# A routed SwiGLU layer on one core: in positions of 64 seats, the down product one block later and the gated tile's halves half a block later

## The chip, the cores and the metric

The kernel runs on one core of a Trainium2 chip. The metric is the device time in microseconds of that core, the median of several runs. The engines are TensorE (PE; its weight loads are PEld), VectorE (DVE), ScalarE (ACT), GpSimd (POOL) and SyncE (SP), which issues the weight loads from HBM.

## The reference

Two layers of an encoder on 256 tokens of width 1024, in f32. The second layer ends in a mixture of experts, and this is where the change lies:

```python
def swiglu(h, w1, w3, w2):
    return (jax.nn.silu(h @ w1) * (h @ w3)) @ w2

def moe_swiglu(h, w_router, w1, w3, w2):
    logits = (h @ w_router).astype(jnp.float32)
    top_v, top_i = lax.top_k(logits, TOP_K)          # TOP_K = 2 of 8 experts
    wts = jax.nn.softmax(top_v, axis=-1)
    combine = jnp.sum(jax.nn.one_hot(top_i, N_EXPERTS, dtype=jnp.float32) * wts[..., None], axis=-2)
    out = jnp.zeros_like(h)
    for e in range(N_EXPERTS):
        out = out + combine[..., e:e + 1] * swiglu(h, w1[e], w3[e], w2[e])
    return out
```

Each expert has w1 and w3 of 1024 x 3584 and w2 of 3584 x 1024, 42 MB together, and all eight are read once.

## The kernel before

**Precision.** Every weight and every activation is split in two f32r parts: a high part (rounded) and a low part (what is left). A product is then three: high x high, low activation x high weight, high activation x low weight. The weights stream through 1 MB items: SP loads an item into one of seven slots of `raw`, ScalarE copies it to `whi` (L1727, "the split"), VectorE subtracts to `wlo` (L2352, "the low part"). `whi` and `wlo` have three slots each. ScalarE may split item n when TensorE is done with item n-3, and SP may load into a slot when VectorE has made the low part of the item that was in it.

**Positions and blocks.** The eight experts are worked on in eight positions, with the roles "HLHLHLHH". A heavy position (H) has 128 seats (rows of tokens); a light one (L) has 64, and goes to an expert with few tokens. In a light position the high and the low part of the rows lie side by side in the 128 columns of one tile. So one pass with the high weights does two products at once, and the sum of the two halves is made later by a matmul with `fold`. Each position has seven blocks (`NM` = 7) of 512 columns of the hidden width. A block has six items: w1 (two halves), w3 (two halves), w2 (two halves).

**One block on the engines.** TensorE (`blocks`) does the up product with w1 of block b into bank 0 (L1188 with the high part of the weights, L1192 with the low part), then `hidden_T` of block b-1, then the up product with w3 of block b into bank 1, then `down` of block b-1 (L1231) into banks 4 and 5. `hidden_T` brings the hidden tile of a block to the layout that the down product wants: in heavy positions by transposes (L1211), in light ones by matmuls with `fold` (L1207) which also add the halves. ScalarE copies bank 0 to SBUF (L1738: silu in heavy positions, plain in light ones). VectorE makes the product with bank 1 in heavy positions (L2366) or copies bank 1 (L2363) in light ones.

In light positions the gate is formed after the fold, so there are four more small steps per block on the tile of 128 x 256: silu (ScalarE, `silu_folded`, L1743), the gated product (VectorE, L2377), its high part (ScalarE, L1749) and its low part (VectorE, L2380; the trace names its output yT_hi, which holds both parts). There is one `silu_t` and one `gated_t`; `gated_m`, where the parts go, has two buffers, taken in turn by blocks. In heavy positions the parts are made straight from the bank (L1753, L2385).

**What sets the order.** Each engine runs the order written out for it in its own section; there is no planner at run time. Items come in the order of `e_items`: `head_items` (w1 and w3 of block 0), `mid_items` (w1, w3 of block b and w2 of block b-1), and w2 of the last block, which comes behind the head of the next position. On ScalarE and VectorE, `e_hi(e_room(...))` and `e_lo(e_room(...))` put ahead of a small step just those items whose slot is free before TensorE reaches the named product. ScalarE also gathers and stores: at block 4 it issues the load of the next position's rows (L1794), VectorE and ScalarE split these rows at block 6 (L1763, L2397), and the result of a position goes out from ScalarE (L1777); after a light position it is folded first, in block 1 of the next (L1243, L1771). An overflow loop, which runs only where an expert has more tokens than its seats, uses the heavy form and did not run here.

Of the kernel before, what the change touches and what calls it, by code (L numbers as in the profile page):

```python
# [33 lines left out]
F32 = mybir.dt.float32  # L34
# [212 lines left out]
def build(nc, x, mem, positions, g_mix, w_in, g_q, g_kv, w_uq, w_uk, w_uv, g_sg, w_s, b_s, g_mem,  # L247
# [31 lines left out]
    with ExitStack() as ctx:  # L279
# [284 lines left out]
            return w[0, :, b, half, :, :, :][e, :, :, :].rearrange("k p c -> p k c")  # L564


        def halves(p, *blocks):
            return [(p, kind, b, half) for kind, b in blocks for half in range(2)]

        def head_items(p):  # L570
            return halves(p, ("w1", 0), ("w3", 0))

        def mid_items(p):
            return [i for b in range(1, NM) for i in halves(p, ("w1", b), ("w3", b), ("w2", b - 1))]

        e_items = head_items(0)
        for p in range(NE):
            e_items += mid_items(p) + (head_items(p + 1) if p < LAST else []) + halves(p, ("w2", NM - 1))
        N_E = len(e_items)
        PER_E = N_E // NE  # L580
        HEAD = len(head_items(0))
# [96 lines left out]
        def e_room(phase, kind, n):  # L678

            limit = marks[phase, kind, n][0]  # L680
            start, end = (N_E, N_E + PER_E) if phase == "over" else (0, N_E)
            i = start + SPLIT
            while i < end and marks["item", i - SPLIT][0] < limit:
                i += 1
            return i
# [13 lines left out]
        def _(pe):  # L699
# [464 lines left out]
                k = 2 if e_items[n][1] == "w2" else 4  # L1164
                return tile[:, (E0 + n) % SPLIT, :].rearrange("p (k c) -> p k c", k=k)

            def is_light(phase):
                return phase != "over" and light[phase]

            def up(phase, kind, b_, j=0, rows=None):  # L1170

                name = {"w1": "e1", "w3": "e3"}[kind]
# [81 lines left out]
            def blocks(phase, j=0):  # L1254

                for b_ in range(1, NM):
                    up(phase, "w1", b_, j)
                    if b_ == 1 and phase != "over" and phase and light[phase - 1]:
                        fold_result(phase - 1)
                    hidden_T(phase, b_ - 1, j)  # L1260
                    if phase != "over" and phase < LAST and b_ == NM - 1:

                        pe.wait_ge(slots_moved, 32 * phase + 16)
                        rows_T(phase + 1)
                    up(phase, "w3", b_, j)
                    if phase == LAST and b_ == NM - 1:
                        down(phase, b_ - 1, j, (0,))
                        hidden_T(phase, b_, j)
                        down(phase, b_ - 1, j, (1,))
                    else:  # L1270
                        down(phase, b_ - 1, j)
                    if phase == LAST and b_ == 2:
                        select_T(phase, j)

# [26 lines left out]
            for p in range(NE):  # L1301
                blocks(p)
                if p < LAST:
                    up(p + 1, "w1", 0, 0, lambda half: read(pe, (p + 1, "rows", half)))
                    hidden_T(p, NM - 1)
                    up(p + 1, "w3", 0)
                    down(p, NM - 1)
            combine(LAST)
            marks["over"] = [count, 0]
# [168 lines left out]
        def _(act):  # L1478
# [239 lines left out]
            def e_hi(end, j=0):  # L1718

                nonlocal n_done  # L1720
                for n in range(n_done, end):
                    act.wait_ge(raw_in[n % RAW], e_base[n % RAW] + 16 * (n // RAW + 1) + 16 * (PER_E // RAW) * j)
                    if N_E <= n < N_E + SPLIT:
                        reached(act, "over", j)
                    else:
                        reached(act, ("item", n - SPLIT), j)
                    nc.scalar.activation(whi[:, (E0 + n) % SPLIT, :], raw[:, n % RAW, :], ACT.Copy).then_inc(hi_ready, 1)  # L1727
                n_done = max(n_done, end)

            def is_light(phase):  # L1730
                return phase != "over" and light[phase]

            def e_silu(phase, b_, j=0):

                b = full(act, (phase, "e1", b_), j)
# [43 lines left out]
            def blocks(phase, j=0):  # L1779

                for b_ in range(1, NM):
                    e_hi(e_room(phase, "e1", b_), j)
                    if is_light(phase):
                        e_hi(e_room(phase, "eT", b_ - 1), j)
                        silu_folded(phase, b_ - 1)
                    e_silu(phase, b_, j)
                    if b_ == 1 and phase != "over" and phase and light[phase - 1]:
                        store_result(phase - 1)
                    if phase != "over" and phase < LAST and b_ == 4:

                        act.wait_ge(dispatched, 16 * 2 * T)
                        if phase:
                            reached(act, (phase, "rows", 1))
                        act.dma_start(row_in_slot, rows_by_slot[phase + 1]).then_inc(slots_moved, 16)  # L1794
                    e_hi(e_room(phase, "eT", b_ - 1), j)
                    hidden_hi(phase, b_ - 1, j)
                    if phase == LAST and b_ == 3:
                        select_T(phase, j)

# [20 lines left out]
            for p in range(NE - 1):  # L1820
                blocks(p)

                e_hi(e_room(p, "e3", NM - 1))
                reached(act, (p, "e3", NM - 1))
                rows_hi_part(p + 1)
                e_hi(e_room(p + 1, "e1", 0))
                if light[p]:
                    e_hi(e_room(p, "eT", NM - 1))
                    silu_folded(p, NM - 1)
                e_silu(p + 1, 0)  # L1830
                e_hi(e_room(p, "eT", NM - 1))
                hidden_hi(p, NM - 1)
                e_hi(e_room(p, "ey", 0))

                act.wait_ge(slots_moved, 32 * p + 16)
                for n in range(2):
                    b = full(act, (p, "ey", n))
                    free(nc.scalar.activation(y_slot[:, n * HALF:(n + 1) * HALF], b[:, :], ACT.Copy), (p, "ey", n))
                if not light[p]:
                    store_result(p)  # L1840
# [25 lines left out]
        def _(dve):  # L1866
# [486 lines left out]
                                    ALU.subtract).then_inc(lo_ready, 1)  # L2353
                n_done = max(n_done, end)

            def is_light(phase):
                return phase != "over" and light[phase]

            def hidden(phase, b_, j=0):

                b = full(dve, (phase, "e3", b_), j)
# [3 lines left out]
                read(dve, (phase, "e1", b_), j)  # L2365
                free(V.tensor_tensor(g32_m, silu_m, b[:, :], ALU.mult), (phase, "e3", b_))  # L2366

            def hidden_lo(phase, b_, j=0):

                end = N_E + PER_E if phase == "over" else N_E  # L2370
                last = phase in (LAST, "over") and b_ == NM - 1
                e_lo(min(e_room(phase, "eT", b_), end - 1 if last else end), j)
                b = full(dve, (phase, "eT", b_), j)
                count = NM * (NE if phase == "over" else phase) + b_ + 1 + NM * j
                if is_light(phase):
                    dve.wait_ge(silu_t_ready, light_block(phase, b_))
                    free(V.tensor_tensor(gated_t, silu_t, b[:, BM * LIGHT:2 * BM * LIGHT], ALU.mult), (phase, "eT", b_))  # L2377
                    dve.wait_ge(g_hi, count)
                    part = by_slot(gated_m[0][:, b_ % 2, :])
                    V.tensor_tensor(part[:, :, LIGHT:2 * LIGHT], gated_t.rearrange("p (c s) -> p c s", c=BM),  # L2380
                                    part[:, :, 0:LIGHT].bitcast(F32), ALU.subtract).then_inc(g_lo, 1)
                    return
                dve.wait_ge(g_hi, count)
                part = [v[:, b_ % 2, :] for v in gated_m]
                free(V.tensor_tensor(part[1], b[:, :], part[0].bitcast(F32), ALU.subtract), (phase, "eT", b_))  # L2385

# [33 lines left out]
            def blocks(phase, j=0):  # L2420

                for b_ in range(1, NM):
                    e_lo(e_room(phase, "e1", b_), j)
                    hidden_lo(phase, b_ - 1, j)
                    e_lo(e_room(phase, "e3", b_), j)
                    if phase != "over" and phase < LAST and b_ == NM - 1:
                        rows_lo(phase + 1)
                    hidden(phase, b_, j)
                    if phase == LAST and b_ == 1:
                        last_choice()  # L2430
                    if phase == LAST and 2 <= b_ <= 5:
                        add_picked(b_ % T, (b_ - 2) // T)
# [22 lines left out]
            for p in range(NE - 1):  # L2455
                blocks(p)
                e_lo(e_room(p + 1, "e1", 0))
                hidden_lo(p, NM - 1)
                e_lo(e_room(p + 1, "e3", 0))
                hidden(p + 1, 0)  # L2460
            dve.wait_ge(flag_ready, 1)
            overflow = dve.value_load(more[0:1, 0:1], min_val=0, max_val=1)
            blocks(LAST)
# [67 lines left out]
```

## Time and profile before

| | |
|---|---|
| median of 3 runs | 1665.05 us (1664.66 to 1665.84) |
| profiled execution | 1664.9 us |
| its span | 1663.1 us |
| PE busy | 1582.4 us (95%) |
| DVE busy | 1286.1 us (77%) |
| ACT busy | 1054.5 us (63%) |
| loaded and stored by DMA | 497.48 MB, mean 299 GB/s |
| weight items of the routed layer | 336 of 1 MB, about 720 us to the end |

The span is the time from the first to the last instruction; the execution lies around it. Busy PE is modelled: matmuls overlap, so a busy engine is not one at its peak. The three light positions lie at about 827 to 945, 1063 to 1181 and 1299 to 1418 us of the span.

### The profile page before, as it was taken

To read this page: it belongs to the slowest core of one execution; us is meant where nothing else is said; L and a number is where in the kernel's file an instruction comes from. 1 tells how busy PE (TensorE), PEld (TensorE's weight loads), DVE (VectorE), ACT (ScalarE), POOL (GpSimd) and SP (SyncE) were. 2 spreads that over 40 slices of the span, in tenths; PEclk is the share of its full clock that TensorE was granted. 3 is DMA by queue.
4 is the path that set the end of the run, shared out by engine and by line. 5 is a ranking of instruction groups with operands and counts; after the bars stand their busy time and mean duration, and the time that the engine had idled before them with its cause. 6 is when DMAs were issued, how large, how long until landed. Compare 5 with 4: busy or idle time off the path is not lost.

```text
span 1663.1 us, 21020 instructions
## 1 busy us (share of the span) xinstructions
PE 1582.4 (95%) x8224; PEld 1332.9 (80%) x8224; DVE 1286.1 (77%) x1204; ACT 1054.5 (63%) x988; POOL 32.4 (2%) x69
## 2 busy tenths in 40 slices
PE   9999999999999999999987999888999888999997
PEld 8988889999899888878766788766788667788885
DVE  7575667555567747698988888898888888888997
ACT  6554436433465544567777777777777777777775
POOL 1000000000000000020000000000000000000100
PEclk9999999999999999999999999999999999999998
DMA  7753488886365444699999999999999999999993
GB/s 234 242 180 121 151 278 282 269 264 190 103 200 198 139 139 165 253 350 409 379 388 396 371 386 388 375 375 404 370 380 374 393 383 384 381 389 366 389 404 121
DMA packets 186120, 497.48 MB, mean 299 GB/s; under 512 B 8534, under 2 KB 64400, under 8 KB 186016
## 3 DMA queue, kind: packets, MB, share of 16 engines
q1 hardware_dynamic: 180016, 479.23, 78.5%
q0 software_dynamic: 2624, 8.45, 1.5%
q10 hardware_dynamic: 3376, 8.39, 1.3%
q8 instruction: 68, 1.11, 0.3%
q14 instruction: 36, 0.29, 0.1%
HBM read 476.64 MB, written 19.40 MB: 298 GB/s over the span
## 4 chain that ended last, share of the span: by engine, by line
PE 65%; DVE 22%; ACT 6%; issue 4%; DMA 1%; SPq 0%; ACTq 0%; POOL 0%; DVEq 0%; POOLq 0%
PE bank L731 20%; DVE wlo L2352 16%; PE bank L1188 12%; PE bank L1231 12%; PE bank L902 9%; PE bank L1192 6%; ACT whi L1727 3%; ACT whi L1494 1%; PE bank L721 1%; DVE wlo L1908 1%; PE bank L1016 1%; PE bank L1211 1%; DMA x_sb<-in_x 1%; DVE sgv L2363 1%; DMA hn<-in_mem 1%
## 5 line engine op out<-in xcount | busy, mean ns | idle before, releaser
L2352 DVE TENSOR_TENSOR wlo<-raw,whi 128x2048 fp32r<-128x2048 f32 x328 | 740.8, 2286 | 96.7 <-ACT whi L1727 96.0
L1727 ACT ACTIVATE whi<-raw 128x2048 fp32r<-128x2048 f32 x328 | 621.6, 1914 | 141.4 <-PE bank L1231 69.3
L1908 DVE TENSOR_TENSOR wlo<-raw,whi 128x2048 fp32r<-128x2048 f32 (+3 forms) x121 | 259.2, 2147 | 176.1 <-ACT whi L1494 174.1
L1188 PE MATMUL bank<-whi,yT_hi 128*128 128x512 f32 x896 | 312.6, 397 | 0.0
L1494 ACT ACTIVATE whi<-raw 128x2048 fp32r<-128x2048 f32 (+3 forms) x121 | 217.7, 1801 | 141.9 <-PE bank L731 100.8
L1192 PE MATMUL bank<-wlo,yT_hi 128*128 128x512 f32 x896 | 243.5, 394 | 4.1 <-DVE wlo L1908 2.8
L1231 PE MATMUL bank<-whi,yT_hi 128*128 128x512 f32 x448 | 180.1, 402 | 57.5 <-DVE wlo L2352 30.7
L1188 PE MATMUL bank<-whi,yT_lo 128*128 128x512 f32 x560 | 217.2, 391 | 0.0
L1192 PEld LDWEIGHTS bank<-wlo,yT_hi 128*128 128x128 f32 x896 | 166.0, 188 | 48.7 <-DVE wlo L2352 10.5
L1188 PEld LDWEIGHTS bank<-whi,yT_hi 128*128 128x128 f32 x896 | 167.0, 188 | 33.4
L1231 PE MATMUL bank<-wlo,yT_hi 128*128 128x512 f32 x448 | 175.8, 392 | 0.0
L1231 PEld LDWEIGHTS bank<-whi,yT_hi 128*128 128x128 f32 x448 | 84.3, 188 | 93.1 <-ACT whi L1727 33.2
L731 PE MATMUL bank<-hT_hi,whi 128*128 128x256 f32 x464 | 131.4, 283 | 0.0
L731 PE MATMUL bank<-hT_hi,wlo 128*128 128x256 f32 x464 | 131.3, 283 | 0.0
L731 PE MATMUL bank<-hT_lo,whi 128*128 128x256 f32 x464 | 131.3, 283 | 0.0
L1188 PEld LDWEIGHTS bank<-whi,yT_lo 128*128 128x128 f32 x560 | 105.5, 189 | 21.3 <-DVE yT_lo L2291 0.2
L1231 PE MATMUL bank<-whi,yT_lo 128*128 128x512 f32 x280 | 109.0, 389 | 0.0
L1231 PEld LDWEIGHTS bank<-wlo,yT_hi 128*128 128x128 f32 x448 | 84.6, 189 | 16.8
L731 PEld LDWEIGHTS bank<-hT_lo,whi 128*128 128x128 f32 x464 | 89.0, 192 | 0.4
L731 PEld LDWEIGHTS bank<-hT_hi,whi 128*128 128x128 f32 x464 | 89.0, 192 | 0.4
L731 PEld LDWEIGHTS bank<-hT_hi,wlo 128*128 128x128 f32 x464 | 89.0, 192 | 0.0
L731 PE MATMUL bank<-whi,mT_hi 128*128 128x512 f32 (+1 forms) x204 | 79.6, 390 | 0.1
(323 smaller groups left out, 2065.9 us busy)
## 6 DMA issues: line engine op xcount, KB each, us to landing
raw<-in_moe_w SPq DMA_DIRECT2D x336, 1024.0 KB, 7.0
raw<-in_w_in SPq DMA_DIRECT2D x36, 1024.0 KB, 5.2
raw<-in_dense_w SPq DMA_DIRECT2D x30, 1024.0 KB, 6.5
raw<-in_w_br SPq DMA_DIRECT2D x12, 1024.0 KB, 5.0
rows_by_slot<-qxT SPq DMA_DIRECT2D x23, 512.0 KB, 7.3
raw<-in_w_out SPq DMA_DIRECT2D x8, 1024.0 KB, 5.0
raw<-in_w_mkv SPq DMA_DIRECT2D x6, 1024.0 KB, 8.3
cqkv<-rows_by_slot ACTq DMA_DIRECT2D x7, 512.0 KB, 6.9
```

Of the source, the lines that this page charges most:

```text
L721: ins = nc.tensor.matmul(bank, lhs(k), rhs(k), start=(k == 0), stop=(k == n - 1))
L731: ins = nc.tensor.matmul(bank, lhs(a, k), rhs(b, k), start=(start and k == chunks[0] and a + b == 0), stop=(stop and k == chunks[-1] and a ...
L902: ins = nc.tensor.matmul(bank, src(a, x0), w[b_][:, w0, :], start=(start and q + i == 0), stop=(stop and last))
L1016: ins = nc.tensor.matmul(b[:, t * SEQ:(t + 1) * SEQ], qT[0:QK, h, tok(t)], kT[0:QK, h, :], start=True, stop=True)
L1188: nc.tensor.matmul(b[:, :], hselT[a][:, half, tok(k)], w[:, k, :], start=(half + k + a == 0), stop=False)
L1192: ins = nc.tensor.matmul(b[:, :], hselT[0][:, half, tok(k)], w[:, k, :], start=False, stop=(half == 1 and k == 3))
L1211: ins = nc.tensor.transpose(b[:, tok(c)], g32_m[:, tok(c)], ident[:, :])
L1231: ins = nc.tensor.matmul(banks[4 + n][:, :], gated_m[a][:, b_ % 2, tok(2 * half + c)], w[p][:, c, n * HALF:(n + 1) * HALF], start=(b_ + ha ...
L1494: nc.scalar.activation(whi[:, m % SPLIT, 0:floats(n)], raw[:, pieces[n][1], 0:floats(n)], ACT.Copy).then_inc(hi_ready, 1)
L1727: nc.scalar.activation(whi[:, (E0 + n) % SPLIT, :], raw[:, n % RAW, :], ACT.Copy).then_inc(hi_ready, 1)
L1908: V.tensor_tensor(wlo[:, m % SPLIT, 0:size], raw[:, pieces[n][1], 0:size], whi[:, m % SPLIT, 0:size].bitcast(F32), ALU.subtract).then_inc( ...
L2352: V.tensor_tensor(wlo[:, s, :], raw[:, n % RAW, :], whi[:, s, :].bitcast(F32), ALU.subtract).then_inc(lo_ready, 1)
```

## The change

Everything is in light positions. The items of w2 come one block later in `e_items`: w2(b-2) behind w1(b) and w3(b), and at the end of the position w2(5) and w2(6) behind the head of the next. TensorE follows: `down` of block b-2 at the end of block b, none at the end of block 1, and two at the end of the position. On ScalarE the high part of the gated tile of block b-2 is made in block b, behind the splits of w1 and w3 and ahead of the silu of block b-1. On VectorE `hidden_lo` is taken apart: `gated_lo` (the low part) of block b-2 is made in block b behind the low parts of w1 and w3, and `gated` (the product) of block b-1 at the end of block b, ahead of the copy of bank 1. The number of instructions and their shapes stay as they were. `is_light` is moved up, so that all engines share it.

```diff
         def mid_items(p):
-            return [i for b in range(1, NM) for i in halves(p, ("w1", b), ("w3", b), ("w2", b - 1))]
+            lag = 2 if is_light(p) else 1
+            return [i for b in range(1, NM)
+                    for i in halves(p, ("w1", b), ("w3", b), *([("w2", b - lag)] if b >= lag else []))]
+
+        def tail_items(p):
+            return halves(p, *([("w2", NM - 2)] if is_light(p) else []), ("w2", NM - 1))
...
-            e_items += mid_items(p) + (head_items(p + 1) if p < LAST else []) + halves(p, ("w2", NM - 1))
+            e_items += mid_items(p) + (head_items(p + 1) if p < LAST else []) + tail_items(p)
...
@@ TensorE, blocks
-                    else:
+                    elif not is_light(phase):
                         down(phase, b_ - 1, j)
+                    elif b_ > 1:
+                        down(phase, b_ - 2)
@@ TensorE, end of a position
                     up(p + 1, "w3", 0)
+                    if light[p]:
+                        down(p, NM - 2)
                     down(p, NM - 1)
@@ ScalarE, blocks
                     if is_light(phase):
-                        e_hi(e_room(phase, "eT", b_ - 1), j)
+                        if b_ > 1:
+                            hidden_hi(phase, b_ - 2)
+                        e_hi(e_room(phase, "eT", b_ - 1))
                         silu_folded(phase, b_ - 1)
...
-                    hidden_hi(phase, b_ - 1, j)
+                    if not is_light(phase):
+                        hidden_hi(phase, b_ - 1, j)
@@ ScalarE, end of a position
                 if light[p]:
+                    hidden_hi(p, NM - 2)
                     e_hi(e_room(p, "eT", NM - 1))
                     silu_folded(p, NM - 1)
                 e_silu(p + 1, 0)
-                e_hi(e_room(p, "eT", NM - 1))
+                e_hi(e_room(p + 1, "e3", 0) if light[p] else e_room(p, "eT", NM - 1))
                 hidden_hi(p, NM - 1)
@@ VectorE
+            def gated(p, b_):
+
+                b = full(dve, (p, "eT", b_))
+                dve.wait_ge(silu_t_ready, light_block(p, b_))
+                if light_block(p, b_) > 1:
+                    dve.wait_ge(g_lo, light_block(p, b_) - 1)
+                free(V.tensor_tensor(gated_t, silu_t, b[:, BM * LIGHT:2 * BM * LIGHT], ALU.mult), (p, "eT", b_))
+
+            def gated_lo(p, b_):
+
+                dve.wait_ge(g_hi, NM * p + b_ + 1)
+                part = by_slot(gated_m[0][:, b_ % 2, :])
+                V.tensor_tensor(part[:, :, LIGHT:2 * LIGHT], gated_t.rearrange("p (c s) -> p c s", c=BM),
+                                part[:, :, 0:LIGHT].bitcast(F32), ALU.subtract).then_inc(g_lo, 1)
@@ VectorE, blocks
                     e_lo(e_room(phase, "e1", b_), j)
-                    hidden_lo(phase, b_ - 1, j)
+                    if not is_light(phase):
+                        hidden_lo(phase, b_ - 1, j)
+                    elif b_ > 1:
+                        gated_lo(phase, b_ - 2)
                     e_lo(e_room(phase, "e3", b_), j)
                     if phase != "over" and phase < LAST and b_ == NM - 1:
                         rows_lo(phase + 1)
+                    if is_light(phase):
+                        gated(phase, b_ - 1)
                     hidden(phase, b_, j)
@@ VectorE, end of a position
                 e_lo(e_room(p + 1, "e1", 0))
-                hidden_lo(p, NM - 1)
+                if light[p]:
+                    gated_lo(p, NM - 2)
+                else:
+                    hidden_lo(p, NM - 1)
                 e_lo(e_room(p + 1, "e3", 0))
+                if light[p]:
+                    gated(p, NM - 1)
                 hidden(p + 1, 0)
+                if light[p]:
+                    gated_lo(p, NM - 1)
```

## Rows read from the trace of the kernel before

**Rows 1.** The page and the groups of instructions: busy, mean ns, idle before
```profile
span 1663.1 us, 21020 instructions
PE 1582.4 (95%) x8224; PEld 1332.9 (80%) x8224; DVE 1286.1 (77%) x1204; ACT 1054.5 (63%) x988; POOL 32.4 (2%) x69
...
L1727 ACT ACTIVATE whi<-raw 128x2048 fp32r<-128x2048 f32 x328 | 621.6, 1914 | 141.4 <-PE bank L1231 69.3 <-PE bank L1192 66.8 <-issue 1.8
```

**Rows 2.** Timeline of VectorE, one light block: start, duration, instruction, [idle before it]
```profile
861.35 0.68 DVE L2363 COPY sgv<-bank 128x512 f32<-128x512 f32 x1
861.95 11.09 DVE L2352 TENSOR_TENSOR wlo<-raw,whi 128x2048 fp32r<-128x2048 f32 x5
872.96 0.41 DVE L2377 TENSOR_TENSOR cT<-cT,bank 128x256 f32<-128x256 f32 x1
873.85 0.43 DVE L2380 TENSOR_TENSOR yT_hi<-cT,yT_hi 128x256 fp32r<-128x256 f32 x1 [0.48 <-ACT yT_hi L1749]
875.66 2.29 DVE L2352 TENSOR_TENSOR wlo<-raw,whi 128x2048 fp32r<-128x2048 f32 x1 [1.38 <-ACT whi L1727]
...
889.47 0.41 DVE L2377 TENSOR_TENSOR cT<-cT,bank 128x256 f32<-128x256 f32 x1
```

**Rows 3.** Timeline of ScalarE in the same block
```profile
867.78 1.91 ACT L1727 ACTIVATE whi<-raw 128x2048 fp32r<-128x2048 f32 x1 [0.26 <-PE bank L1192]
869.60 0.36 ACT L1743 ACTIVATE cT<-bank 128x256 f32<-128x256 f32 x1
...
873.40 0.42 ACT L1749 ACTIVATE yT_hi<-cT 128x256 fp32r<-128x256 f32 x1 [2.95 <-DVE cT L2377]
```

**Rows 4.** Timeline of TensorE in the same block, from w1 half 1 on
```profile
866.49 1.19 PE L1192 MATMUL bank<-wlo,yT_hi 128*128 128x512 f32 x4
867.52 1.89 PE L1207 MATMUL bank<-cT,sgv 128*128 128x64 f32 x16
...
871.16 1.08 PE L1188 MATMUL bank<-whi,yT_hi 128*128 128x512 f32 x4
...
874.33 0.50 PE L1231 MATMUL bank<-whi,yT_hi 128*128 128x512 f32 x1 [1.19 <-DVE yT_hi L2380]
```

**Rows 5.** The group of L2380 over the whole span
```profile
L2380 DVE TENSOR_TENSOR yT_hi<-cT,yT_hi 128x256 fp32r<-128x256 f32 x21 | 8.9, 425 | 10.1 <-ACT yT_hi L1749 10.1
```

**Rows 6.** Windows: length, busy (instructions) by engine, PEclk, DMA share, GB/s
```profile
717.00:734.00 17.00, 17.00 (x78) 14.06 (x77) 14.96 (x9) 12.68 (x9) 1.51 (x1) 1.00 1.02 417
734.00:751.00 17.00, 17.00 (x79) 14.05 (x78) 14.95 (x9) 12.67 (x9) 0.00 (x0) 1.00 1.03 410
...
853.00:870.00 17.00, 14.11 (x67) 10.89 (x66) 15.14 (x10) 12.74 (x12) 0.00 (x0) 1.00 1.00 366
```

**Rows 7.** Timeline of VectorE, one heavy block, from its L2385 to the next
```profile
740.28 0.68 DVE L2385 TENSOR_TENSOR yT_lo<-bank,yT_hi 128x512 fp32r<-128x512 f32 x1
...
757.08 0.68 DVE L2385 TENSOR_TENSOR yT_lo<-bank,yT_hi 128x512 fp32r<-128x512 f32 x1
```

**Rows 8.** Timeline of VectorE, start of the first light position
```profile
833.31 6.70 DVE L2352 TENSOR_TENSOR wlo<-raw,whi 128x2048 fp32r<-128x2048 f32 x3 [1.49 <-ACT whi L1727]
```

**Rows 9.** Timeline of VectorE, block 6 of the first light position
```profile
927.41 1.28 DVE L2397 TENSOR_TENSOR yT_lo<-bank,yT_hi 128x512 fp32r<-128x512 f32 x2
```

**Rows 10.** Timeline of TensorE, end of the first light position
```profile
927.64 0.47 PE L1231 MATMUL bank<-whi,yT_hi 128*128 128x512 f32 x1 [1.65 <-DVE wlo L2352]
...
929.56 0.40 PE L1188 MATMUL bank<-whi,yT_hi 128*128 128x512 f32 x1
...
939.85 0.39 PE L1188 MATMUL bank<-whi,yT_hi 128*128 128x512 f32 x1
...
942.57 0.39 PE L1231 MATMUL bank<-whi,yT_hi 128*128 128x512 f32 x1
...
947.28 0.39 PE L1188 MATMUL bank<-whi,yT_hi 128*128 128x512 f32 x1
```

**Rows 11.** Weight loads issued between 820 and 828 us
```profile
DMA to landing us min/median/max: 6.8/7.1/7.9
```

More of the change, by code:

```diff
@@ L564, in e_source, with is_light @@
             return w[0, :, b, half, :, :, :][e, :, :, :].rearrange("k p c -> p k c")
+        def is_light(phase):
+            return phase != "over" and light[phase]
         def halves(p, *blocks):
@@ L1165, in e_part @@
                 return tile[:, (E0 + n) % SPLIT, :].rearrange("p (k c) -> p k c", k=k)
-            def is_light(phase):
-                return phase != "over" and light[phase]
             def up(phase, kind, b_, j=0, rows=None):
@@ L1728, in e_hi @@
                 n_done = max(n_done, end)
-            def is_light(phase):
-                return phase != "over" and light[phase]
             def e_silu(phase, b_, j=0):
@@ L2354, in e_lo @@
                 n_done = max(n_done, end)
-            def is_light(phase):
-                return phase != "over" and light[phase]
             def hidden(phase, b_, j=0):
@@ L2373, in hidden_lo @@
                 b = full(dve, (phase, "eT", b_), j)
[L2374 to L2383, printed above, removed]
+                dve.wait_ge(g_hi, NM * (NE if phase == "over" else phase) + b_ + 1 + NM * j)
                 part = [v[:, b_ % 2, :] for v in gated_m]
```

## The prediction

> **What bounds the kernel now.** I read the page first: 1663.1 us of span, TensorE busy 95% [rows 1]. That is a mean over stages. Then I read the VectorE timeline of one block of a 64-seat position, because the change touches only those. The reader sees there, per block, six low-part instructions, a copy, the gated product (L2377) and its low part (L2380), and two pauses: 0.48 us before L2380 and 1.38 us before the next low part [rows 2]. From the gated product to the next one it is 16.51 us (872.96 to 889.47). The work in it is 6 x 2.202 (11.01 for five, start to start) + 0.60 + 0.41 + 0.43 = 14.65 us, and the pauses are the other 1.86.
>
> The ScalarE timeline says why [rows 3]: it stands 2.95 us before L1749, for L2377; then comes 0.42 of high part and then a weight split of 1.9 us, for which VectorE waits. Nothing else holds that split: TensorE had been done with the item three before it since 871.2 [rows 4]. So two engines hand one tile to and fro in order, and the next weight item queues behind it on ScalarE. TensorE stands too, 1.19 us for L2380 [rows 4] and 1.65 us for the low part (the same wait stands first in [rows 10]), once each per block: here it follows, it does not set the pace. The pattern is the same 21 times; L2380's wait sums to 10.1 us [rows 5]. In positions of 128 seats TensorE is busy for the whole of a 17 us window [rows 6] and a block takes 16.80 us [rows 7], so these set their own pace and hand on any gain of a light position unshortened.
>
> **The change part by part.** Nothing is added or removed in number: 42 items per position, the same products, the same three small tiles per block. Moved are, in light positions: the down product of block b to block b+2's end, L2380's counterpart to half a block later, ScalarE's high part the same, and the gated product to the end of the block. SP's loads follow the new item order, one for one; POOL has nothing here.
>
> *Steady block.* VectorE would run: 4 low parts, low part of g(b-2), 2 low parts, gated product of b-1, copy of b. ScalarE's high part of g(b-2) now needs a product that VectorE made at the end of the block before, so it never waits; the 2.95 and both pauses go. Three followers could be late next. (a) The gated product needs the silu of the folded tile: ready at 869.96 in this block [rows 3], needed after the sixth low part, at about 875.6: hidden. (b) The split of the sixth item, w2 half 1, needs TensorE done with w3 half 0. The low part of w1 half 1 ends at 861.95 + 2 x 2.202 = 866.35; TensorE then does its last quartet, the fold, and w3 half 0, done at 871.16 [rows 4]; ScalarE starts 0.26 after such an end (867.52 to 867.78) and takes 1.92: 873.34. VectorE wants it after 3 low parts and one small one, at 866.35 + 6.61 + 0.43 = 873.39. Slack 0.05 us: it fits and no more. I price it at nothing; the other end is a wait per block of whatever the estimate misses, for which the nearest row is a handoff of 0.26, 15 blocks, 4 us. (c) The ring of raw slots, below. TensorE is busy 14.1 us of 17 in such blocks [rows 6], or 13.7 of 16.51, which fits in 14.65. So a steady block takes 14.65.
>
> *Start of a light position.* Up to the three low parts at 833.31 nothing changes [rows 8]. Then w3(1) twice and w1(2) twice end at 833.31 + 8.81 = 842.12; gated 0, copy 1: 843.13; w3(2) twice, low part of g(0), w2(0) twice: 852.37; gated 1, copy 2: 853.38. Three blocks: copy 5 ends at 897.3. The low part of w2(4) half 1 ends at 897.3 + 13.21 + 0.43 = 911.0. Before, the same place in the code (last low part ahead of the two row parts, L2397) ended at 927.41 [rows 9]; 16.4 earlier, with two items fewer done, 4.40, and one small instruction.
>
> *End of a light position.* TensorE started the second half of the down product at 927.64, 0.15 us after its low part, and the next position's w1 at 929.56 [rows 10]. After: 911.1 and 913.0, 16.5 earlier. Up products and fold of a 128-seat head then run with no gap on TensorE, 929.56 to 942.57 = 13.0 us, so to 926.0. Now two more halves of down product stand here, w2(5): VectorE's low part of the first is done at 911.0 + 1.2 (rows) + 0.41 + 0.60 + 8.81 + 0.43 + 2.2 = 924.6, that of the second, whose split must wait for w3' half 0 (939.85 - 16.5 = 923.3) and takes 1.92, at 927.6; TensorE does both by 929.8. The last gated product keeps the old handoff: gated 6 at 927.6 to 928.0, ScalarE's high part to 928.4, and only then its split of w2(6) half 0, to 930.3; low part to 932.6. The product of the next position's block 0 and the low part of g(6), 1.03 us, lie inside that wait. TensorE stands from 929.8 to 932.7 (2.9 us), does half 0 to 934.6, waits 0.3 for half 1 and ends at 936.8. Before, this point was 947.28 [rows 10]. **Gain 10.4 us per light position, 31.2 for three**: of 7 x 1.86 = 13.0 us of pauses per position about 2.6 stay or come back at the end. Bounds: 6 x 1.86 = 11.2 if the end costs only its pause, so 33.6 in all; and 8 if that end costs a further low part of 2.3.
>
> *The loads.* A light block moves 6 x 1.0486 = 6.29 MB; in 14.65 us that asks 429 GB/s. With many loads under way, in the stretch from 717 on, the rows show 417 and 410 GB/s [rows 6], so a block alone would need 6.29 / 0.410 = 15.3 us. The ring of seven slots can cover this for a time. From 827.1 (two low parts, 2 x 2.3, ahead of the 1.49 us of wait in [rows 8]) to 911.0 VectorE frees 34 slots; with a result store and a row load of 0.52 MB that is 36.7 MB in 83.8 us; at 410 GB/s it takes 89.5. Loads fall behind by 5.7 us. A load landed in 7.1 us when the position began [rows 11] and may take 14.65 - 1.94 - 0.2 = 12.5 before ScalarE is late (a slot is wanted again one block later, less the split). 7.1 + 5.7 = 12.8: the ring runs dry just as the position ends, 0.3 us short. The next position, at TensorE's pace (6.29 MB in 16.8 us, 374 GB/s), fills it again. At 417 it is never dry; at 405, my lower guess between rows, 1.4 us per position. I take 0.3 x 3 = 1 us, range 0 to 4.5.
>
> The page DMA: Bandwidth & Descriptors of the Trainium skill (Where 436 GB/s comes from) says that loads from HBM are held by the HBM side at about 358 GB/s per core. The rows contradict it for this core alone: 410 over a whole window [rows 6]. Another section of that page (Bandwidth) has 425 GB/s for one core alone and large transfers; by it an estimate is 36.7 / 0.425 = 86.4 us and a ring that never dries, 1 us better than my sum.
>
> **Sum**: 31.2 - 1 = 30.2 us. The profiled execution took 1664.9 us (1.8 outside its span), the median of the runs is 1665.05, 0.15 more, which changes nothing; so 1664.9 - 30.2 = **1634.7 us**, 1.8% less.
>
> **Rivals.**
> A. *The chain of (b) is late.* Each block then waits for its sixth split. For it: slack of 0.05 us only. Against: every time in it is a row of an undisturbed block. Price 0.3 to 1.0 us x 15 blocks: 1639 to 1650, at its middle 1644.
> B. *The loads take the place of the pauses.* If the ring gives less cover than I reckon (bursts with gaps), all of 15.3 per block stands: 0.7 x 15 = 10 us back, 1645, and with the store and the row load up to 5.7 x 3 = 17, 1651. For it: the loads' share is full in all windows. Against: of the 141.4 us that ScalarE's splits waited, 137.9 are put down by name and none to a load [rows 1], and the ring held landings of 7 us where 12.5 are allowed.
> C. *Slower than before.* In the window 853 to 870 the rate was 366 GB/s at a full share [rows 6]. Were that what the memory gives to this order of loads, and not what was asked for, 36.7 MB would take 100.3 us against 83.8, 16.5 lost against 10.4 won, and 128-seat blocks (6.29 / 0.366 = 17.2 us) would not refill the ring: 1665 + 3 x 6 = 1683. It decides below 36.7 / (83.8 + 10.4) = 390 GB/s. Against: 410 to 417 held from 717 to 751, two blocks. The 358 GB/s of the Trainium skill's page would have this effect too.
> D. *The change does nothing*: the high part waits as before, because the new order on VectorE meets the old point on ScalarE. Price 0: 1665. Against: the code puts the product a half block and four splits ahead of its reader.
>
> **How the numbers follow.** Forecast (31 us within a few) 0.70; A 0.10; B 0.12; C 0.04; D 0.02; 0.02 for something unnamed on either side. Low end: 33.6 won and no load wait, 1631.4, less 1.4 for sizes: 1630. High end: takes in most of B and the middle of A, 1647. 0.2% of 1665 is 3.3 us, about what a measurement here tells from no change. Faster: forecast, A, B and half the unnamed, 0.93; same: D and a part of C, 0.03; slower: 0.04.
>
> **What would show it.** Right: in light positions VectorE's timeline shows six low parts, gated, copy in 14.65 us, no wait before L2380's counterpart, no wait of ScalarE for the gated product except at the end of the position; there TensorE waits some 2.9 us before the last down product (and the end of its last down product, at 947.28 [rows 10], moves to 936.8). Landings grow through a light position to 11 or 12 us. Wrong: a wait of VectorE for the sixth split (A), ScalarE waiting for raw (B or C), 128-seat blocks over 16.8 us.

## The result and the profile after

The changed kernel takes 1638.67 us in the median (1636.11 to 1639.41, 4 runs) against 1665.44 us for the kernel before, measured alongside it: a ratio of 0.9837, 95% interval 0.982 to 0.9854, 26.8 us less. I had said 1634.7 and 1630 to 1647. The traced execution has a span of 1636.6 us against 1663.1.

The VectorE timeline of a light block, answering [rows 2] (start, duration, instruction, [idle before]; L2362 is the low part of a weight item, L2381 the gated product, L2387 its low part, L2370 the copy of bank 1):

```profile
865.03 0.42 DVE L2381 TENSOR_TENSOR cT<-cT,bank 128x256 f32<-128x256 f32 x1
865.36 0.69 DVE L2370 COPY sgv<-bank 128x512 f32<-128x512 f32 x1
865.96 8.89 DVE L2362 TENSOR_TENSOR wlo<-raw,whi 128x2048 fp32r<-128x2048 f32 x4
874.76 0.42 DVE L2387 TENSOR_TENSOR yT_hi<-cT,yT_hi 128x256 fp32r<-128x256 f32 x1
875.10 4.55 DVE L2362 TENSOR_TENSOR wlo<-raw,whi 128x2048 fp32r<-128x2048 f32 x2
879.56 0.41 DVE L2381 TENSOR_TENSOR cT<-cT,bank 128x256 f32<-128x256 f32 x1
```

No row has an idle time: both pauses of [rows 2] are gone, and a block takes 14.53 us (865.03 to 879.56) where it took 16.51. My figure was 14.65. A block of a 128-seat position behind it takes 16.82 us (967.64 to 984.46, both at L2398, VectorE's low part there), as before.

What is left stands in block 6 and at the end of a position. The same timeline, answering [rows 9], then ScalarE's last high part, which answers to the 2.95 us of [rows 3]:

```profile
907.29 2.29 DVE L2362 TENSOR_TENSOR wlo<-raw,whi 128x2048 fp32r<-128x2048 f32 x1 [0.82 <-ACT whi L1736]
909.50 1.28 DVE L2410 TENSOR_TENSOR yT_lo<-bank,yT_hi 128x512 fp32r<-128x512 f32 x2
...
924.49 2.29 DVE L2362 TENSOR_TENSOR wlo<-raw,whi 128x2048 fp32r<-128x2048 f32 x1 [1.44 <-ACT whi L1736]
926.70 0.42 DVE L2381 TENSOR_TENSOR cT<-cT,bank 128x256 f32<-128x256 f32 x1
927.03 0.68 DVE L2373 TENSOR_TENSOR sgv<-sgv,bank 128x512 f32<-128x512 f32 x1
927.63 0.42 DVE L2387 TENSOR_TENSOR yT_hi<-cT,yT_hi 128x256 fp32r<-128x256 f32 x1
929.41 6.70 DVE L2362 TENSOR_TENSOR wlo<-raw,whi 128x2048 fp32r<-128x2048 f32 x3 [1.36 <-ACT whi L1736]
```
```profile
927.15 0.42 ACT L1755 ACTIVATE yT_hi<-cT 128x256 fp32r<-128x256 f32 x1 [2.69 <-DVE cT L2381]
```

TensorE's timeline at the end of the first light position, answering [rows 10] (L1236 is the down product; L1193 at 938.40 is the first matmul of the up product that follows), and the same place in the second:

```profile
931.84 0.77 PE L1236 MATMUL bank<-whi,yT_hi 128*128 128x512 f32 x1 [2.82 <-DVE wlo L2362]
932.41 0.63 PE L1236 MATMUL bank<-wlo,yT_hi 128*128 128x512 f32 x1
...
938.40 0.39 PE L1193 MATMUL bank<-whi,yT_hi 128*128 128x512 f32 x1
...
1161.34 0.47 PE L1236 MATMUL bank<-whi,yT_hi 128*128 128x512 f32 x1 [2.82 <-DVE wlo L2362]
1161.65 0.40 PE L1236 MATMUL bank<-wlo,yT_hi 128*128 128x512 f32 x1
...
1165.47 0.39 PE L1193 MATMUL bank<-whi,yT_hi 128*128 128x512 f32 x1
```

The wait is 2.82 us; the working gave 2.9. But what follows it takes 6.56 us in the first position (931.84 to 938.40) and 4.13 in the second, for the same sixteen matmuls. The windows (columns as in [rows 6]) show why: in the first, TensorE's granted clock was 0.50, the lower of its two levels.

```profile
932.00:936.00 4.00, 4.00 (x10) 3.13 (x11) 4.00 (x2) 1.28 (x2) 0.00 (x0) 0.50 1.03 411
...
1162.00:1166.00 4.00, 3.87 (x18) 2.88 (x17) 4.00 (x3) 2.96 (x4) 0.00 (x0) 1.00 1.03 411
```

**Where the 26.5 us of the two traces are.** A mark in both is the first low part behind the wait of 1.48 or 1.49 us in block 1 of a light position (833.31 before, [rows 8]) and, behind the third position, the one after a wait of 3 us. Before, the last three of the four marks:

```profile
1069.60 6.70 DVE L2352 TENSOR_TENSOR wlo<-raw,whi 128x2048 fp32r<-128x2048 f32 x3 [1.48 <-ACT whi L1727]
...
1305.81 6.70 DVE L2352 TENSOR_TENSOR wlo<-raw,whi 128x2048 fp32r<-128x2048 f32 x3 [1.48 <-ACT whi L1727]
...
1430.22 2.29 DVE L2352 TENSOR_TENSOR wlo<-raw,whi 128x2048 fp32r<-128x2048 f32 x1 [3.10 <-ACT whi L1727]
```

After, all four:

```profile
831.58 8.90 DVE L2362 TENSOR_TENSOR wlo<-raw,whi 128x2048 fp32r<-128x2048 f32 x4 [1.49 <-ACT whi L1736]
...
1060.66 8.90 DVE L2362 TENSOR_TENSOR wlo<-raw,whi 128x2048 fp32r<-128x2048 f32 x4 [1.48 <-ACT whi L1736]
...
1287.72 8.90 DVE L2362 TENSOR_TENSOR wlo<-raw,whi 128x2048 fp32r<-128x2048 f32 x4 [1.48 <-ACT whi L1736]
...
1403.79 2.29 DVE L2362 TENSOR_TENSOR wlo<-raw,whi 128x2048 fp32r<-128x2048 f32 x1 [3.04 <-ACT whi L1736]
```

The lead grows from 1.73 to 8.94, 18.09 and 26.43 us: 7.2, 9.15 and 8.3 us per light position, 24.7 in all. The first 1.73 lie ahead of anything that the change touches. TensorE's clock was granted at 0.89 in 706 to 722 us of the trace before and at 1.00 in that of after. The control e6 below is the changed kernel run once more. It has 0.89 there again, and its first mark lies at 833.22 us, so these 1.73 us belong to the execution and not to the change. Its marks:

```profile
833.22 8.90 DVE L2362 TENSOR_TENSOR wlo<-raw,whi 128x2048 fp32r<-128x2048 f32 x4 [1.49 <-ACT whi L1736]
...
1059.95 8.90 DVE L2362 TENSOR_TENSOR wlo<-raw,whi 128x2048 fp32r<-128x2048 f32 x4 [1.48 <-ACT whi L1736]
...
1287.92 8.90 DVE L2362 TENSOR_TENSOR wlo<-raw,whi 128x2048 fp32r<-128x2048 f32 x4 [1.49 <-ACT whi L1736]
...
1404.01 2.29 DVE L2362 TENSOR_TENSOR wlo<-raw,whi 128x2048 fp32r<-128x2048 f32 x1 [3.20 <-ACT whi L1736]
```

Here the three positions give 9.56, 8.24 and 8.32 us, 26.1 in all.

### The profile page after: what moved, and what is told of

The parts are those of the page before. It is cut to its first block, busy times and chain, and to the rows that moved or that the text cites. A ratio compares the mean times of both kernels' runs of the same rounds, so it can differ in the third digit from the quotient of the medians.

```text
span 1636.6 us, 21020 instructions
## 1 busy us (share of the span) xinstructions
PE 1585.5 (97%) x8224; PEld 1334.3 (82%) x8224; DVE 1284.8 (79%) x1204; ACT 1057.1 (65%) x988; POOL 31.9 (2%) x69
## 4 chain that ended last, share of the span: by engine, by line
PE 71%; DVE 18%; ACT 5%; issue 4%; DMA 2%; ACTq 0%; POOL 0%; DVEq 0%; SPq 0%; POOLq 0%
PE bank L739 21%; PE bank L1193 14%; PE bank L1236 13%; DVE wlo L2362 12%; PE bank L910 9%; PE bank L1197 8%; ACT whi L1736 2%; ACT whi L1503 1%; PE bank L729 1%; DVE wlo L1918 1%; PE bank L1024 1%; DMA raw<-in_moe_w 1%; PE bank L1216 1%; PE bank L1212 1%; DVE sgv L2370 1%
## 5 line engine op out<-in xcount | busy, mean ns | idle before, releaser
L2362 DVE TENSOR_TENSOR wlo<-raw,whi 128x2048 fp32r<-128x2048 f32 x328 | 742.6, 2287 | 82.3 <-ACT whi L1736 81.5
L1736 ACT ACTIVATE whi<-raw 128x2048 fp32r<-128x2048 f32 x328 | 625.3, 1917 | 166.2 <-PE bank L1197 76.5
L1193 PE MATMUL bank<-whi,yT_hi 128*128 128x512 f32 x896 | 312.0, 396 | 0.0
L1193 PE MATMUL bank<-whi,yT_lo 128*128 128x512 f32 x560 | 216.5, 390 | 0.0
L1236 PE MATMUL bank<-whi,yT_hi 128*128 128x512 f32 x448 | 181.0, 404 | 26.3 <-DVE wlo L2362 20.7
L1193 PEld LDWEIGHTS bank<-whi,yT_hi 128*128 128x128 f32 x896 | 166.7, 188 | 33.3
L1236 PE MATMUL bank<-wlo,yT_hi 128*128 128x512 f32 x448 | 177.3, 396 | 0.0
L1236 PEld LDWEIGHTS bank<-whi,yT_hi 128*128 128x128 f32 x448 | 85.7, 191 | 59.8 <-issue 29.7
L1193 PEld LDWEIGHTS bank<-whi,yT_lo 128*128 128x128 f32 x560 | 105.2, 188 | 21.2 <-DVE yT_lo L2301 0.2
L1236 PE MATMUL bank<-whi,yT_lo 128*128 128x512 f32 x280 | 109.0, 389 | 0.0
L1236 PEld LDWEIGHTS bank<-wlo,yT_hi 128*128 128x128 f32 x448 | 85.7, 191 | 17.2
```

The costliest lines, as they stand in the source:

```text
L1193: nc.tensor.matmul(b[:, :], hselT[a][:, half, tok(k)], w[:, k, :], start=(half + k + a == 0), stop=False)
L1236: ins = nc.tensor.matmul(banks[4 + n][:, :], gated_m[a][:, b_ % 2, tok(2 * half + c)], w[p][:, c, n * HALF:(n + 1) * HALF], start=(b_ + ha ...
L2362: V.tensor_tensor(wlo[:, s, :], raw[:, n % RAW, :], whi[:, s, :].bitcast(F32), ALU.subtract).then_inc(lo_ready, 1)
```

## The experiments

Theory H: what went is a handoff. VectorE's gated product, ScalarE's high part and VectorE's low part follow each other in order, and ScalarE's next split is queued behind the high part. Rival P: what went is TensorE's wait for the down product. For the part of the forecast that is missing, the candidates are the loads (L) and TensorE's clock (K). The experiments are called e1 to e8.

**e1: the down product late, alone.** ScalarE and VectorE keep the order they had before; items and TensorE have the new one.

```diff
@@ ScalarE, light block
-                        if b_ > 1:
-                            hidden_hi(phase, b_ - 2)
...
-                    if not is_light(phase):
-                        hidden_hi(phase, b_ - 1, j)
+                    hidden_hi(phase, b_ - 1, j)
...
@@ VectorE, light block
-                    elif b_ > 1:
-                        gated_lo(phase, b_ - 2)
+                    else:
+                        e_lo(e_room(phase, "eT", b_ - 1))
+                        gated(phase, b_ - 1)
+                        gated_lo(phase, b_ - 1)
...
-                    if is_light(phase):
-                        gated(phase, b_ - 1)
...
```

> Only the down product is one block later (and its items and the two at the end); the gated product, its high part and its low part stay together at the place they had in the kernel before. Theory H (the gain is the handoff between VectorE and ScalarE, with the next split queued behind the high part): VectorE still pauses 0.48 and 1.38 us per block, a light block stays at 16.5 us, and the time is that of before, 1663 to 1668 us. Theory P (the gain is that TensorE no longer waits 1.19 and 1.65 us for the down product): most of the gain is there, 1640 to 1648 us.

The same is done at the end of a position (not shown).

Measured: 1676.55 us, ratio 1.0066 (1.005 to 1.0081). Theory P falls. H had the pauses right, but neither the time nor the block: it is slower than before, and a block such as the one from 868.28 to 885.52 us takes 17.24 us instead of 16.5. The timelines of VectorE and TensorE:

```profile
885.52 0.42 DVE L2377 TENSOR_TENSOR cT<-cT,bank 128x256 f32<-128x256 f32 x1
886.42 0.42 DVE L2383 TENSOR_TENSOR yT_hi<-cT,yT_hi 128x256 fp32r<-128x256 f32 x1 [0.48 <-ACT yT_hi L1755]
888.23 2.29 DVE L2358 TENSOR_TENSOR wlo<-raw,whi 128x2048 fp32r<-128x2048 f32 x1 [1.38 <-ACT whi L1736]
...
896.46 2.29 DVE L2358 TENSOR_TENSOR wlo<-raw,whi 128x2048 fp32r<-128x2048 f32 x1 [0.94 <-ACT whi L1736]
```
```profile
890.67 0.77 PE L1236 MATMUL bank<-whi,yT_hi 128*128 128x512 f32 x1 [2.83 <-DVE wlo L2358]
891.23 0.63 PE L1236 MATMUL bank<-wlo,yT_hi 128*128 128x512 f32 x1
```

The pauses of 0.48 and 1.38 us are there as before. TensorE, whose two waits were 1.19 and 1.65 us [rows 4, 10], now has one of 2.83, about the same in sum. Behind it matmuls lie 0.43 us apart instead of 0.23, and the split that waits for them comes late (0.94). All eleven waits of 2.5 to 2.9 us ahead of the down product in this trace have such slow matmuls behind them, and the mean granted clock of the whole run is 0.982 against 0.995 before. So e1 is not the down product's delay alone: it brings a fall of the clock with it. What it shows is that the delay doesn't remove VectorE's pauses. What the delay would cost or give at the full clock no run shows.

**e2: the late split first, and nothing else.** The kernel before with two lines changed:

```diff
-                    e_hi(e_room(phase, "eT", b_ - 1), j)
+                    e_hi(e_room(phase, "eT", b_ - 1) + is_light(phase), j)
                     hidden_hi(phase, b_ - 1, j)
...
-                e_hi(e_room(p, "eT", NM - 1))
+                e_hi(e_room(p, "eT", NM - 1) + light[p])
                 hidden_hi(p, NM - 1)
```

> The kernel before with one edit: in light positions ScalarE makes one more split (the one that was late) ahead of the high part of the gated tile; nothing is moved on TensorE, VectorE or SP. The slot for it is free in time by the trace of before (871.4 us, the gated product comes at 873.4). Theory H: the pause of 1.38 us goes in all seven handoffs of a position, that of 0.48 stays, a block takes 15.13 us; 1.38 x 21 = 29.0 us less, 1636 to 1640 us, as good as the changed kernel, since at 416 GB/s the loads ask less of the ring. Theory P: TensorE's down product still waits for the low part, so little goes, 1655 us or more.

Measured: 1641.1 us, ratio 0.9854 (0.9839 to 0.9869). So 24.8 us come from one split moved ahead of the high part on ScalarE. VectorE's timeline:

```profile
885.45 0.42 DVE L2377 TENSOR_TENSOR cT<-cT,bank 128x256 f32<-128x256 f32 x1
886.35 0.43 DVE L2380 TENSOR_TENSOR yT_hi<-cT,yT_hi 128x256 fp32r<-128x256 f32 x1 [0.48 <-ACT yT_hi L1749]
886.69 2.28 DVE L2352 TENSOR_TENSOR wlo<-raw,whi 128x2048 fp32r<-128x2048 f32 x1
...
900.50 0.41 DVE L2377 TENSOR_TENSOR cT<-cT,bank 128x256 f32<-128x256 f32 x1
...
917.09 0.43 DVE L2380 TENSOR_TENSOR yT_hi<-cT,yT_hi 128x256 fp32r<-128x256 f32 x1 [1.13 <-ACT yT_hi L1749]
...
934.59 0.42 DVE L2380 TENSOR_TENSOR yT_hi<-cT,yT_hi 128x256 fp32r<-128x256 f32 x1 [1.74 <-ACT yT_hi L1749]
```

A block takes 15.05 us; 1.38 is gone and 0.48 stays, as expected. In the last two handoffs of a position VectorE waits 1.13 and 1.74 us for the high part, 1.91 more than twice 0.48. In three positions that is 5.7 us, enough for the miss of 1 to 5 us.

**e3: the same at the end of the changed kernel's positions.**

```diff
-                e_hi(e_room(p + 1, "e3", 0) if light[p] else e_room(p, "eT", NM - 1))
+                e_hi(e_room(p + 1, "e3", 0) + 1 if light[p] else e_room(p, "eT", NM - 1))
                 hidden_hi(p, NM - 1)
```

> The changed kernel with one edit: at the end of a light position ScalarE makes the split of w2(6) half 0 ahead of the high part of the last gated tile. VectorE's pause of 1.36 us there goes, and TensorE's wait of 2.82 us falls to 1.4. If the last handoff is what keeps the gain at 9 instead of 13 us per position: 1.4 x 3 = 4.3 us less than the changed kernel, and some more if TensorE's clock no longer falls behind the shorter wait (it cost 2.7 and 1.0 us in two of three positions): a ratio to before of 0.9790 to 0.9815, some 1631 to 1635 us. If the loads bound the end of the position (ScalarE then waits for raw instead): no difference from the changed kernel, 1636 to 1639.

Measured: 1632.25 us, ratio 0.9803 (0.9789 to 0.9816), better than the changed kernel. VectorE's pause of 1.36 us is gone, and TensorE waits half as long, without a fall of the clock (1.00 in the windows over all three ends):

```profile
932.37 0.47 PE L1236 MATMUL bank<-whi,yT_hi 128*128 128x512 f32 x1 [1.38 <-DVE wlo L2362]
```

**e4: half of each load.**

```diff
-                sp.dma_start(dst, src).then_inc(raw_in[slot], 16)
+                half = src.shape[1] // 2
+                sp.dma_start(dst[:, :half, :], src[:, :half, :]).then_inc(raw_in[slot], 16)
```

> The changed kernel, but each weight load of the routed layer from position 0 on brings only half of its rows per partition (0.5 MB instead of 1), so that the rest of the slot holds old data; all engines do the same work. Theory L (the loads take back part of the gain at the ends of light positions): ScalarE's waits for raw, 14.8 us in sum in the trace of the changed kernel, go to 0, and 2 to 4 us of time go with them: 1634.5 to 1637. If the loads were hidden even so: no difference, within 1 us of the changed kernel's 1638.7. Were it more than 6 us, my account of the ring would be wrong.

Measured: 1637.93 us, ratio 0.9831 (0.9818 to 0.9845) beside 0.9837: no difference that can be told. In the changed kernel ScalarE does wait for loads, 14.8 us in sum. The loads issued between 1055 and 1140 us, in the second light position, landed in 12.0 us in the median and 13.6 at most, where my working allowed 12.5:

```profile
DMA to landing us min/median/max: 7.6/12.0/13.6
```

ScalarE's splits in the changed kernel, then here:

```profile
L1736 ACT ACTIVATE whi<-raw 128x2048 fp32r<-128x2048 f32 x328 | 625.3, 1917 | 166.2 <-PE bank L1197 76.5 <-PE bank L1236 69.4 <-DMA raw<-in_moe_w 14.8
```
```profile
L1737 ACT ACTIVATE whi<-raw 128x2048 fp32r<-128x2048 f32 x328 | 624.8, 1917 | 165.7 <-PE bank L1197 87.3 <-PE bank L1236 73.1 <-issue 1.6
```

The sum of its waits is the same, 166.2 and 165.7 us. Without the loads it waits for TensorE instead: 145.9 us in the changed kernel (76.5 for the up product and 69.4 for the down product) and 160.4 here. VectorE's pause ahead of the sixth low part of block 6 is still there:

```profile
909.27 2.29 DVE L2363 TENSOR_TENSOR wlo<-raw,whi 128x2048 fp32r<-128x2048 f32 x1 [0.81 <-ACT whi L1737]
```

**e5 and e6: the clock kept up.** Ten idle matmuls in the wait at the end of a light position, and the changed kernel again as a control (e6).

```diff
                         down(p, NM - 2)
+                        for _ in range(10):
+                            nc.tensor.matmul(banks[3][:, 0:P], ident[:, :], ident[:, :], start=True, stop=True)
                     down(p, NM - 1)
```

> The changed kernel with ten more matmuls of 128 columns on TensorE (result unused, into a bank that lies idle) in the wait of 2.8 us ahead of the last down product of each light position. Theory K (that wait brings TensorE's granted clock to its lower level in some positions, 2.7 us lost in the first and 1.0 in the third of the traced run): the granted clock stays 1.00 in 926 to 940 and its like, no matmul of the last down product is 0.43 us apart, and the time is 1 to 3.5 us under the changed kernel in the same call. Theory N (the fall of the clock is not tied to the wait): the clock falls as before and the time is the same or some tenths longer.

> The changed kernel once more, as the control of this call: 1636 to 1639.5 us. What its trace shows of TensorE's clock after the 2.8 us waits tells whether it falls in the same positions each time.

Measured: 1636.46 us (0.9817, 0.9803 to 0.983) against 1638.84 for the control (0.9837, 0.9824 to 0.9851). The intervals overlap, so the 2.4 us alone settle little; the traces say more. The granted clock over the three ends (924 to 944, 1150 to 1172, 1376 to 1400 us) is 1.00, 1.00, 1.00 with the matmuls, 1.00, 0.92, 0.93 in the control and 0.83, 1.00, 0.93 in the first trace of the changed kernel. The second position, with the matmuls and in the control (the granted clock is the third number from the end):

```profile
1150.00:1172.00 22.00, 21.27 (x107) 17.46 (x107) 18.76 (x12) 16.25 (x13) 0.00 (x0) 1.00 1.03 409
```
```profile
1150.00:1172.00 22.00, 19.18 (x75) 14.77 (x74) 17.63 (x11) 14.96 (x11) 0.00 (x0) 0.92 1.03 409
```

With e4 there are nine waits of 2.8 us that stand empty; the clock fell behind six of them, and behind none of the three that the matmuls filled. So the fall is tied to the wait but does not follow every one. In the traced run of e5 VectorE also paused 1.7 and 1.6 us, in bits of 0.2 to 0.5, in blocks 4 to 6 of its first two light positions. In the first of them ScalarE waited for loads:

```profile
ACT whi L1738 <- DMA raw<-in_moe_w: 7.6, 12, 1.9
```

These are 7.6 us in twelve waits between 870 and 915 us, the longest 1.9. So the loads can reach VectorE in one execution and not in another: in the control each light position has only the one pause in block 6 (0.69, 0.58 and 0.81 us).

**e7: the rows' transposes later**, on top of the split at the end.

```diff
-                    if phase != "over" and phase < LAST and b_ == NM - 1:
+                    if phase != "over" and phase < LAST and b_ == NM - 1 and not light[phase]:
...
                     up(phase, "w3", b_, j)
+                    if is_light(phase) and b_ == NM - 1:
+                        pe.wait_ge(slots_moved, 32 * phase + 16)
+                        rows_T(phase + 1)
```

> The changed kernel with the split ahead at the end (as in e3_end_split) and, in light positions, the eight transposes of the next position's rows (0.80 us on TensorE) behind the up product with w3 of block 6 instead of ahead of it. Theory R (the 0.82 us pause of VectorE before the sixth low part of block 6 is my tight chain (b) with these transposes in it): the pause goes, 0.8 x 3 = 2.4 us under e3_end_split, 1629.5 to 1630.5 us at 1665.4 of before. If the pause is the loads (ScalarE waits 0.3 to 0.65 us for raw just there): it stays, and so does the time of e3_end_split, 1632 us.

Measured: 1629.71 us, ratio 0.9787 (0.9774 to 0.9801), 36 us under before and the shortest of the kernels that load all of their weights. The pause ahead of the sixth low part of block 6 is gone; in the first light position (L2413 are the row parts, and the wait of 1.44 us at the end of the position stays):

```profile
906.13 4.55 DVE L2365 TENSOR_TENSOR wlo<-raw,whi 128x2048 fp32r<-128x2048 f32 x2
910.60 1.28 DVE L2413 TENSOR_TENSOR yT_lo<-bank,yT_hi 128x512 fp32r<-128x512 f32 x2
...
925.59 2.29 DVE L2365 TENSOR_TENSOR wlo<-raw,whi 128x2048 fp32r<-128x2048 f32 x1 [1.44 <-ACT whi L1739]
```

The intervals of e3 and e7 overlap, so the traces decide: mark to mark, the three light positions are 0.93, 0.72 and 0.77 us shorter than in e3, 2.4 in all, as Theory R had it.

**e8: and that with half loads**, to see if the loads bind at this pace.

> The kernel of e7_rows_later, but each weight load of the routed layer brings only half of its rows per partition (0.5 MB), so that the rest of the slot holds old data. e7 asks the loads for more than the changed kernel does (its light positions are 2.2 us shorter). Theory L2 (at this pace the ring of slots begins to run dry in some executions, as the spread of e7, 1629.6 to 1631.8, suggests): 0.5 to 2 us less, 1628 to 1629, with a narrower spread. If the loads are hidden here too: 1629.5 to 1630.5.

Measured: 1629.07 us, ratio 0.9782 (0.9769 to 0.9796): 0.0005 under e7, which can't be told from none. Theory L2 is neither shown nor excluded.

## Why the prediction was right, and where it was off

*The handoff, and 14.65 us for a steady block*: right, 14.53. e2 shows the cause: with only the split moved ahead of the high part, 24.8 us go. e1 shows that the down product's delay leaves both pauses where they were. In the changed kernel it is what lets the high part be made half a block later.

*(a), the silu hidden*: right, no wait before L2381.

*(b), the sixth split with 0.05 us of slack, priced at nothing*: right in blocks 2 to 5, wrong in block 6. There TensorE makes the next rows' transposes, 0.80 us, inside the chain, and VectorE paused 0.82. I had reckoned the chain from a block without them. That is rival A in one block of seven. e7 takes it away, for 2.4 us in the traces and 2.5 in the medians.

*The end of a position, 2.9 us of wait and 936.8*: the wait came out at 2.82; the end at 938.40, where 936.8 less the 1.73 of the early start is 935.1. Of these 3.3 us, 2.4 are the slow matmuls behind the wait (6.56 us against 4.13), which no step of mine had. The other 0.9 stand ahead of it: the wait ended at 931.84 us, which is 933.6 with the early start, where I had 932.7. That is about what the pause of 0.82 us in block 6 gives; no run separates the two. I had named the wait, and not what a wait does to the clock, though the trace before had an example. There TensorE waited 2.02 us at the start of the first light position, and slow matmuls (0.63 us instead of 0.39) followed:

```profile
841.30 0.50 PE L1231 MATMUL bank<-whi,yT_hi 128*128 128x512 f32 x1 [2.02 <-DVE yT_hi L2380]
...
842.36 0.63 PE L1231 MATMUL bank<-wlo,yT_hi 128*128 128x512 f32 x1
```

*The loads, 1 us and at most 4.5; rivals B and C*: the mechanism is there, landings of 12.0 us in the median of the second position and ScalarE waiting 14.8 us, but on an engine with time in hand. The medians of e4 and e8 lie 0.0006 and 0.0005 of the ratio, about 1 us, under those of the kernels with whole loads, which is within the intervals. In single traces the price differs: the changed kernel's second position gave 9.15 us, with three pauses of 0.26 to 0.29, and the first two of e5 gave 8.07 and 8.11, against 9.51 in its third; in their blocks 4 to 6 ScalarE waited 7.6 and 7.4 us for loads, in the third 3.4. So in that execution the loads took some 1.4 us twice. B is a matter of 0 to 3 us per execution, not of 10. The loads ran at 409 GB/s over the ends of the light positions (windows of 20 to 24 us), so C, which needed less than 390, falls. The limit of about 358 GB/s that the Trainium skill states for loads from HBM (DMA: Bandwidth & Descriptors, Where 436 GB/s comes from) doesn't hold for this core working alone.

*The sum, 31.2 - 1 = 30.2*: 24.7 and 26.1 in the two traces where the change acts, 26.8 in the medians. The term that was mis-sized is the gain per position, 10.4. Where the clock stayed up and VectorE paused in block 6 alone it was 9.5 or 9.6 (9.56 in e6's first position, 9.55 and 9.51 in the third of e4 and e5). Of the 0.85 us that are missing there, the pause in block 6 is 0.8 by e7. Where the clock fell it was 8.2 to 8.3 in five positions and 7.2 in one. That the steady block was 0.1 us shorter than I had it, some 0.5 us per position, worked the other way, so about as much more is lost in a place that no run shows.

## What to carry to other kernels

When two engines pass a tile to and fro, look at what is queued behind the wait on the engine that waits: one split moved ahead of it gave 24.8 us alone where the whole reordering gave 26.8 (the two intervals overlap), and moved ahead at the end of the reordered positions it gave some 6 more. A chain that just fits must be reckoned for the block with the most in it, not for the typical one. A wait of 2 to 3 us on TensorE can cost more than its length, and two shorter waits can be cheaper than one of the same sum (e1 beside the kernel before).

## What the runs showed of the hardware that I had not expected

After a wait of 2.8 us TensorE's granted clock was in some positions at the lower level (0.50 in 932 to 936 us), with matmuls 0.43 us apart instead of 0.23. It was so in two of three positions in each of three traces (the changed kernel, its control and e4), and not in the same ones. The sixteen matmuls behind the wait took 4.13 or 4.14 us where the clock stayed up, 5.33 to 5.35 in five places and 6.56 in one. So a fall cost 1.2 or 2.4 us. After the waits of 1.4 us at the same place (e3, e7, e8) the clock stayed at 1.00 over all three ends. In between nothing is sure: in the kernel before, the same wait of 2.0 us stands at the start of each light position, and the clock fell behind the first (841.30 us) and not behind the other two. In one position of e1 it fell behind two waits of 1.37 and 1.14 us that lay about 1 us apart, and in its other two it did not.
